# Four gated up projections: from 32 direct matmuls a chunk to seven block products, with the weight sums on GpSimd

## The chip, the cores and the metric

The kernel runs on one core of a Trainium2 chip, as one program written engine by engine: TensorE (PE), VectorE (DVE), ScalarE (ACT), GpSimd (POOL) and SyncE (SP) each have their own list of instructions, and they meet only at semaphores. The metric is the time of one execution on the device, in microseconds; lower is better. All arithmetic is in float32.

## The reference, cut to what matters

A sequence of 256 tokens with 1024 features goes through a first block of two layers and a second block of four layers. The change touches the gated feed-forward parts of the first block, two in each layer:

```python
def swiglu(h, w1, w3, w2):      # h: 256 x 1024, w1, w3: 1024 x 2816, w2: 2816 x 1024
    return (silu(h @ w1) * (h @ w3)) @ w2

mod = silu(c) @ w_ada[layer] + b_ada[layer]     # nine vectors of 1024 features
...
x = x + 0.5 * g1 * swiglu(modulate(rmsnorm(x), sh1, sc1), ffn_w1[layer, 0], ffn_w3[layer, 0], ffn_w2[layer, 0])
...                                             # attention
x = x + 0.5 * g3 * swiglu(modulate(rmsnorm(x), sh3, sc3), ffn_w1[layer, 1], ffn_w3[layer, 1], ffn_w2[layer, 1])
```

Each layer of the second block ends in a feed-forward part with a convolution over the gate (three taps). Its up projection has the same sizes.

## The kernel before

**Chunks.** All big weights come from memory in 244 chunks of 128 partitions x 4096 columns (2 MB), in the order of their use, through a ring of four slots. SyncE's queue issues them; the load of chunk c waits until chunk c - 4 is used (`chunks_used`). A chunk of an up projection holds, for eight blocks of 128 input features, 256 columns of w1 (the gate) and 256 columns of w3 (the up part). An up projection has 11 such chunks, j = 0 to 10; the down projection after it has 6.

**Gated stages.** There are four, n = 0 to 3 (`swiglu_pe`, `swiglu_act`, `swiglu_dve`, lines 1265 to 1308), at chunks 0, 26, 43 and 69. For each chunk TensorE multiplies its four column groups by the transposed tokens `hT` (eight blocks of 128 features x 256 tokens): 32 matmuls of 256 columns (`channels_pe`, line 600), into PSUM banks 4 and 5 for even j, 6 and 7 for odd j. The trace shows every float32 matmul as two records, so a chunk is 64. ScalarE takes the gate bank through SiLU into `cbuf` (line 1292), VectorE multiplies it by the up bank into `aT` (line 1308). Chunks 0 and 1 are multiplied token half by token half (128 columns), since the second half of `hT` comes later (`first_channels_pe`).

**Adaptive sums.** silu(c) @ w_ada is computed beside the stages 0, 1 and 2, in 36 pieces of 2 MB. VectorE runs over the eight 512-column blocks of a piece, one scaling and seven multiply-adds into `ada_sum` (lines 220 and 223), each with a wait for the one before. TensorE sums over the partitions with a matmul against ones (`ada_reduce_pe`, lines 231 and 234), and VectorE takes the result from PSUM (`ada_take_dve`, lines 250 to 263). Stages 0 and 1 carry eleven pieces, one a chunk, stage 2 seven, stage 3 none. TensorE reduces piece j - 1 just ahead of chunk j; VectorE sums piece j and takes piece j - 1 before the product of chunk j. The down projections 0 and 2 go on with pieces; they wait at their start until the pieces of the stage are taken (`ada_taken`).

**Stage 3** also normalizes the memory input (`mem_norm_act`, `mem_norm_dve`) at chunk 2 and transposes it on TensorE (`mem_pe`, line 638) at chunk 5.

**Block products elsewhere.** The up projections of the second block already use Strassen's form in Winograd's variant from chunk 2 on (`gated_pe`, lines 2590 to 2626): the chunk is a 2 x 2 matrix of blocks (halves of the input features by gate and up columns), `hT` too (feature halves by token halves), and seven products of 8 matmuls of 128 columns replace eight such products. VectorE forms the sums of weights, four operations of 128 x 1024 a chunk (`gated_left_dve`, lines 2573 to 2578), and adds the products up, seven operations of 128 x 256 (`gated_out_dve`, lines 2632 to 2641). The down projections 3, 5, 8, 11, 14 and the last use the form too (`seven_pe`, line 382).

**GpSimd** only sets up constants at the start and issues a few loads: small weights, gates and the memory (`attn_pool`, `gates_pool`, `mem_pool`, `mamba_pool`).

## Time and profile before

| what | value |
|---|---|
| median of 3 runs | 3718.9 us (3716.49 to 3721.02) |
| span of the profiled execution | 3717.0 us |
| instructions in it | 42263 |
| TensorE busy | 3667.4 us, 99% |
| VectorE busy | 1567.6 us, 42% |
| ScalarE busy | 736.1 us, 20% |
| GpSimd busy | 15.9 us |
| TensorE matmuls at line 600 (direct projections, these and others) | 5568 records, 941.6 us |
| HBM reads | 594.97 MB, 160 GB/s over the span |

The profile is one execution. "Busy" is the union of an engine's instructions; matmul ends are modelled. A line such as `L223 DVE SCALAR_TENSOR_TENSOR memT<-big,silu_c,memT 128x512 f32` names the source line, the engine, the operation, what it writes and reads, and the shape (partitions x elements). `x7` is the number of instructions merged. In the chain of waits each piece of time is put down to the instruction that ended last; when TensorE is 98% of it, the other engines matter only where they make it wait. The profile has no time for the work around the span apart from the runs' times; the median of the runs is 1.9 us above the span of this execution.

### The profile page before, as it was taken

What the parts mean: (1) busy time and instruction counts of PE and PEld (TensorE: products, weight loads), DVE (VectorE), ACT (ScalarE), POOL (GpSimd) and SP (SyncE); (2) the same over time, 40 slices, a digit from 0 to 9 for tenths busy, and PEclk for the clock granted to TensorE, in tenths of its full rate; (3) what the DMA queues carried; (4) which work ended last, traced back from release to release, by engine and by line L of the source; (5) the groups of instructions that cost most, each with busy time, mean ns of one, the idle gap of its engine ahead of it and who ended that gap; (6) DMA issues with size and microseconds to landing.
All of it is one profiled execution on the core that took longest, in us unless ns stands there. A gap on an engine that the chain in (4) does not pass through costs nothing.

```text
span 3717.0 us, 42263 instructions
## 1 busy us (share of the span) xinstructions
PE 3667.4 (99%) x18452; PEld 2737.0 (74%) x18452; DVE 1567.6 (42%) x2772; ACT 736.1 (20%) x1434; POOL 15.9 (0%) x43
## 2 busy tenths in 40 slices
PE   6999999999999999999999999999999999999999
PEld 5856697785668687587957679778657977757795
DVE  5434342334420345223833236736523673432384
ACT  1003400100431044211112111133211113521110
POOL 1000000000000000000000000000000000000000
PEclk9999999999999999999999999999999999999999
DMA  9753476554324442343443334432333444334342
GB/s 398 282 199 136 172 293 242 226 196 167 127 104 159 167 150 108 119 159 125 171 159 132 119 114 168 173 140 110 114 115 113 168 173 159 114 113 159 123 178 102
DMA packets 42472, 598.74 MB, mean 161 GB/s; under 512 B 4736, under 2 KB 4752, under 8 KB 6192
## 3 DMA queue, kind: packets, MB, share of 16 engines
q1 hardware_dynamic: 41024, 589.94, 42.9%
q0 software_dynamic: 1264, 6.10, 0.4%
q8 instruction: 146, 2.39, 0.3%
q14 instruction: 38, 0.31, 0.0%
HBM read 594.97 MB, written 1.05 MB: 160 GB/s over the span
## 4 chain that ended last, share of the span: by engine, by line
PE 98%; issue 1%; DVE 1%; ACT 1%; DMA 0%
PE ps L600 25%; PE ps L2602 12%; PE ps L483 9%; PE ps L382 8%; PE ps L463 5%; PE ps L2060 4%; PE ps L503 3%; PE ps L2093 3%; PE ps L796 3%; PE ps L2502 3%; PE ps L1568 2%; PE ps L1588 2%; PE ps L2829 2%; PE ps L1563 2%; PE ps L813 1%; PE ps L625 1%
## 5 line engine op out<-in xcount | busy, mean ns | idle before, releaser
L600 PE MATMUL ps<-hT,ring 128*128 128x256 f32 (+1 forms) x5568 | 941.6, 331 | 3.6 <-DVE stat L324 3.6
L600 PEld LDWEIGHTS ps<-hT,ring 128*128 128x128 f32 x5568 | 855.1, 191 | 88.1 <-issue 7.7
L483 PE MATMUL ps<-ring,aT 128*128 128x512 f32 x784 | 341.1, 592 | 0.0
L483 PEld LDWEIGHTS ps<-ring,aT 128*128 128x128 f32 x784 | 147.9, 190 | 179.1 <-issue 178.9
L463 PE MATMUL ps<-ring,aT 128*128 128x512 f32 x448 | 196.1, 597 | 0.0
L1308 DVE TENSOR_TENSOR aT<-cbuf,ps 128x512 f32<-128x512 f32 x44 | 30.3, 688 | 374.7 <-ACT cbuf L1292 374.7
L223 DVE SCALAR_TENSOR_TENSOR memT<-big,silu_c,memT 128x512 f32<-128x512 f32 x238 | 179.0, 752 | 8.5
L2060 PE MATMUL ps<-hT,ring 128*128 128x256 f32 x768 | 174.5, 384 | 0.0
L525 ACT ACTIVATE big<-x 128x1024 f32<-128x1024 f32 x34 | 35.9, 1057 | 696.6 <-DVE x L577 389.9
L2060 PEld LDWEIGHTS ps<-hT,ring 128*128 128x128 f32 x768 | 146.8, 193 | 26.7 <-issue 7.7
L463 PEld LDWEIGHTS ps<-ring,aT 128*128 128x128 f32 x448 | 85.1, 191 | 103.6 <-issue 103.5
L1292 ACT ACTIVATE cbuf<-ps 128x512 f32<-128x512 f32 x44 | 26.3, 597 | 579.1 <-PE ps L600 579.1
L2602 PE MATMUL ps<-big 128*128 128x128 f32 x1152 | 140.4, 275 | 0.0
L2602 PE MATMUL ps<-big,ring 128*128 128x128 f32 x1152 | 140.4, 275 | 0.0
L382 PE MATMUL ps<-ring,aT 128*128 128x512 f32 x288 | 135.3, 592 | 0.0
L2602 PE MATMUL ps<-hT,ring 128*128 128x128 f32 x1152 | 134.5, 275 | 0.0
L2602 PEld LDWEIGHTS ps<-big 128*128 128x128 f32 x1152 | 134.4, 192 | 0.0
L2602 PEld LDWEIGHTS ps<-big,ring 128*128 128x128 f32 x1152 | 134.4, 192 | 0.0
L2602 PEld LDWEIGHTS ps<-hT,ring 128*128 128x128 f32 x1152 | 131.5, 192 | 0.0
L2222 DVE SCALAR_TENSOR_TENSOR big<-cbuf,col,big 128x256 f32<-128x256 f32 x192 | 80.3, 480 | 101.9 <-ACT big L2109 100.7
L2093 PE MATMUL ps<-ring,hT 128*128 128x512 f32 x256 | 113.4, 594 | 0.0
L503 PE MATMUL ps<-big,ring 128*128 128x256 f32 x512 | 111.8, 379 | 0.0
(546 smaller groups left out, 4634.9 us busy)
## 6 DMA issues: line engine op xcount, KB each, us to landing
ring<-weights_in SPq DMA_DIRECT2D x244, 2048.0 KB, 7.7
big<-ada_in SPq DMA_DIRECT2D x34, 2048.0 KB, 7.8
ring<-ada_in SPq DMA_DIRECT2D x2, 2048.0 KB, 22.7
big<-b_gate_in POOLq DMA_DIRECT2D x1, 1536.0 KB, 17.3
x<-x_in SPq DMA_DIRECT2D x1, 1024.0 KB, 4.8
big<-b_gate_in POOLq DMA_DIRECT2D x1, 1024.0 KB, 8.9
big<-mem_in POOLq DMA_DIRECT2D x1, 1024.0 KB, 5.5
out<-big SPq DMA_DIRECT2D x2, 512.0 KB, 2.6
```

The source lines that it names most:

```text
L223: dve.scalar_tensor_tensor(out=ada_sum[:, a % 2, :], in0=w[:, k, :], scalar=silu_c[:, k:k + 1], in1=ada_sum[:, a % 2, :], op0=ALU.mult, op ...
L382: last = pe.matmul(ps[:, bank, :], left(2 * j + q), right[:, q, :], start=(j == 0 and q == 0), stop=(j == 3 and q == 1), skip_group_check= ...
L463: last = pe.matmul(ps[:, 2 * t + half, :], aT[:, 4 * j + k, t * P:(t + 1) * P], w[:, k, half * 512:(half + 1) * 512], start=(4 * j + k == ...
L483: last = pe.matmul(ps[:, 2 * t + half, :], aT[:, 4 * c + k, t * P:(t + 1) * P], w[:, k, half * 512:(half + 1) * 512], start=first, stop=(4 ...
L503: last = pe.matmul(ps[:, 4 + 2 * j + m // 2, (m % 2) * SEQ:(m % 2 + 1) * SEQ], w[:, k, m * P:(m + 1) * P], view(big, 0, KT, SEQ)[:, k, :], ...
L600: last = pe.matmul(ps[:, bank + m // 2, (m % 2) * SEQ + at:(m % 2) * SEQ + at + n], w[:, k, m * P:(m + 1) * P], hT[:, k, at:at + n], start ...
L796: last = pe.matmul(ps[:, bank + m // 2, (m % 2) * SEQ:(m % 2 + 1) * SEQ], w[:, k, m * P:(m + 1) * P], hT[:, k, :], start=(k == 0), stop=(k ...
L2060: last = pe.matmul(ps[:, bank + m // 2, (m % 2) * SEQ:(m % 2 + 1) * SEQ], w[:, k, m * P:(m + 1) * P], hT[:, k, :], start=(k == 0), stop=(k ...
L2093: last = pe.matmul(ps[:, 4 + 2 * (j % 2) + t, :], hT[:, k, t * P:(t + 1) * P], w[:, k, :], start=(k == 0), stop=(k == KT - 1))
L2222: last = dve.scalar_tensor_tensor(out=mamba_conv(j)[:, m, :], in0=cbuf[:, j % 2, m, 1 + tap:1 + tap + SEQ], scalar=col[:, w:w + 1], in1=ma ...
L2502: last = pe.matmul(cross_block(place), left[:, k, :], right[:, k, :], start=(k == 0), stop=(k == 3), skip_group_check=True)
L2602: last = pe.matmul(gated_block(j, place)[:, m * P:(m + 1) * P], left[:, k, m * P:(m + 1) * P], right[:, k, :], start=(k == 0), stop=(k == ...
```

## The change

From chunk 2 on, each gated stage uses the seven products. The four sums of weights are on GpSimd (`up_left_pool`), into three single buffers of `big` and in place in the ring; the four sums of `hT` on VectorE once a stage (`up_right_dve`); the sums of products on VectorE, seven operations of 128 x 256 a chunk (`up_out_dve`). ScalarE copies product 1 from PSUM into `cbuf` and takes SiLU of the finished gate in place. The product of gate and up reads both from SBUF. Even chunks use banks 4 to 6 and half of bank 3, odd chunks banks 0 to 2 and the other half of bank 3; bank 7 is for the adaptive reductions. A reduction now stands between the fourth and the fifth product of its chunk and waits until the piece before it is taken (`taken=0`); the take stands behind the sums of the chunk's products, and then comes the sum of the next piece but one. The down projections 0 and 2 wait for the last product of the stage already at their first reduction; down projections 3 and 5 wait for the sums of products of chunk 10 before their third product. The memory's norm comes at the start of stage 3, its transposes before chunk 2. The wait counts of the later stages are shifted for the semaphores that are now shared (gated_left by 144, gated_out by 180, gated_products, seven_tokens); nothing else changes there.

```diff
-        def ada_reduce_pe(pe, a, bank):
+        def ada_bank(bank):
+
+            return ps[:, bank, :]
+
+        def ada_reduce_pe(pe, a, place, taken=1):
 
             pe.wait_ge(ada_step, 8 * a + 8)
             if a >= 4:
-                pe.wait_ge(ada_taken, a - 1)
+                pe.wait_ge(ada_taken, a - taken)
...
                 if j < len(ada):
-                    ada_reduce_pe(pe, ada[j], 6 + ada[j] % 2)
+                    if j == 0:
+                        pe.wait_ge(*then)
+                    ada_reduce_pe(pe, ada[j], ada_bank(6 + ada[j] % 2))
...
+        def up_left_part(i):
+
+            return view(big, 12288 + 1024 * i, 4, SEQ)
+
+        def up_right_part(i):
+
+            return (view(big, 15360, 4, P), view(big, 15872, 4, P), view(gdn_work, 512, 4, P), view(aTf, 5120, 4, P))[i]
+
+        def up_block(j, at):
+
+            if at == 6 and j < 10:
+                return ps[:, 3, SEQ * (1 - j % 2):SEQ * (1 - j % 2) + SEQ]
+            return ps[:, 4 * (1 - j % 2) + at // 2, SEQ * (at % 2):SEQ * (at % 2) + SEQ]
+
+        def up_ada_place(j):
+
+            return ps[:, 7, SEQ:512] if j == 10 else ps[:, 7, :]
...
+        def up_ready(engine, i):
+
+            if i is None:
+                engine.wait_ge(norm_act_done, 5)
+                engine.wait_ge(norm_dve_done, 7)
+            else:
+                engine.wait_ge(down_act_done, 6 * i + 6)
+                engine.wait_ge(down_dve_done, 8 * i + 8)
+
+        def up_left_pool(pool, n, i, c0):
+
+            s1, s2, s4 = (up_left_part(part) for part in range(3))
+            up_ready(pool, i)
+            for j in range(2, 11):
+
+                w = arrived(pool, c0 + j).rearrange("p (k c) -> p k c", k=KT)
+                a11, a12, a21, a22 = w[:, 0:4, 0:SEQ], w[:, 4:8, 0:SEQ], w[:, 0:4, SEQ:512], w[:, 4:8, SEQ:512]
+                if j > 2:
+                    pool.wait_ge(gated_products, up_products_count(n, j - 1, 2))
+                pool.tensor_tensor(s1, a21, a22, ALU.add).then_inc(gated_left, 1)
+                pool.wait_ge(gated_left, up_left_count(n, j, 1))
+                pool.tensor_tensor(a21, a11, a21, ALU.subtract).then_inc(gated_left, 1)
+                if j > 2:
+                    pool.wait_ge(gated_products, up_products_count(n, j - 1, 3))
+                pool.tensor_tensor(s2, s1, a11, ALU.subtract).then_inc(gated_left, 1)
+                if j > 2:
+                    pool.wait_ge(chunks_used, c0 + j)
+                pool.wait_ge(gated_left, up_left_count(n, j, 3))
+                pool.tensor_tensor(s4, a12, s2, ALU.subtract).then_inc(gated_left, 1)
+
+        def up_right_dve(dve, n, i):
+
+            b11, b12, b21, b22 = hT[:, 0:4, 0:P], hT[:, 0:4, P:SEQ], hT[:, 4:8, 0:P], hT[:, 4:8, P:SEQ]
+            t1, t2, t3, t4 = (up_right_part(part) for part in range(4))
+
+            up_ready(dve, i)
+            dve.tensor_tensor(t1, b12, b11, ALU.subtract).then_inc(seven_tokens, 1)
+            dve.tensor_tensor(t3, b22, b12, ALU.subtract).then_inc(seven_tokens, 1)
+            dve.wait_ge(seven_tokens, up_right_count(n) + 1)
+            dve.tensor_tensor(t2, b22, t1, ALU.subtract).then_inc(seven_tokens, 1)
+            dve.wait_ge(seven_tokens, up_right_count(n) + 3)
+            dve.tensor_tensor(t4, b21, t2, ALU.subtract).then_inc(seven_tokens, 1)
+
+        def up_pe(pe, n, c0, j, ada, mem):
+
+            w = arrived(pe, c0 + j).rearrange("p (k c) -> p k c", k=KT)
+            s1, s2, s4 = (up_left_part(part) for part in range(3))
+            t1, t2, t3, t4 = (up_right_part(part) for part in range(4))
+
+            def product(place, left, right):
+                for m in range(2):
+                    for k in range(4):
+                        last = pe.matmul(up_block(j, place)[:, m * P:(m + 1) * P], left[:, k, m * P:(m + 1) * P], right[:, k, :], start=(k == 0), stop=(k == 3), skip_group_check=True)
+                return last
+
+            if j >= 4:
+                pe.wait_ge(gated_out, up_out_count(n, j - 2, 5))
+            elif j == 2:
+                pe.wait_ge(swiglu_dve_done, 11 * n + 1)
+            product(1, w[:, 4:8, 0:SEQ], hT[:, 4:8, 0:P])
+            product(0, w[:, 0:4, 0:SEQ], hT[:, 0:4, 0:P]).then_inc(gated_products, 1)
+            pe.wait_ge(seven_tokens, up_right_count(n) + 4)
+            pe.wait_ge(gated_left, up_left_count(n, j, 1))
+            product(2, s1, t1).then_inc(gated_products, 1)
+            if j == 2:
+                pe.wait_ge(swiglu_dve_done, 11 * n + 2)
+            product(4, w[:, 4:8, SEQ:512], t4)
+            for a in ada:
+                ada_reduce_pe(pe, a, up_ada_place(j), taken=0)
+            pe.wait_ge(gated_left, up_left_count(n, j, 3))
+            product(3, s2, t2).then_inc(gated_products, 1)
+            if j > 2:
+                pe.wait_ge(gated_out, up_out_count(n, j - 1, 4))
+            elif mem:
+                pe.wait_ge(mem_act_done, 4)
+                pe.wait_ge(mem_dve_done, 4)
+            product(6, w[:, 0:4, SEQ:512], t3)
+            pe.wait_ge(gated_left, up_left_count(n, j, 4))
+            product(5, s4, hT[:, 4:8, P:SEQ]).then_inc(chunks_used, 1)
+
+        def up_out_dve(dve, n, c0, j):
+
+            p1, p2, p5, p6, p4, p3, p7 = (up_block(j, at).rearrange("p (m c) -> p m c", m=2) for at in range(7))
+            part, late = view(gdn_work, 0, 2, P), view(gdn_work, 256, 2, P)
+            gate, up = cbuf[:, j % 2, 0:2, 4:260], aT[:, 2 * j:2 * j + 2, :]
+
+            dve.wait_ge(chunks_used, c0 + j + 1)
+            dve.wait_ge(swiglu_act_done, up_act_count(n, j, 1))
+            dve.tensor_tensor(part, gate[:, :, 0:P], p6, ALU.add).then_inc(gated_out, 1)
+            dve.tensor_tensor(gate[:, :, 0:P], gate[:, :, 0:P], p2, ALU.add)
+            dve.wait_ge(gated_out, up_out_count(n, j, 1))
+            dve.tensor_tensor(late, part, p5, ALU.add).then_inc(gated_out, 1)
+            dve.wait_ge(gated_out, up_out_count(n, j, 2))
+            dve.tensor_tensor(gate[:, :, P:SEQ], late, p3, ALU.add).then_inc(gated_out, 1)
+            dve.tensor_tensor(part, part, p7, ALU.add).then_inc(gated_out, 1)
+            dve.wait_ge(gated_out, up_out_count(n, j, 4))
+            dve.tensor_tensor(up[:, :, P:SEQ], part, p5, ALU.add)
+            dve.tensor_tensor(up[:, :, 0:P], part, p4, ALU.add).then_inc(gated_out, 1)
+
         def swiglu_pe(pe, n, i, c0, ada=(), mem=False):
 
             if i is None:
                 pe.wait_ge(norm_dve_done, 8)
+                for j in range(2):
+                    w = arrived(pe, c0 + j).rearrange("p (k c) -> p k c", k=KT)
+                    channels_pe(pe, w, 4 + 2 * j).then_inc(chunks_used, 1)
+            else:
+                first_channels_pe(pe, i, c0)
+            if mem:
+                mem_pe(pe)
+            for a in ada[0:1]:
+                ada_reduce_pe(pe, a, ada_bank(0))
+            for j in range(2, 11):
+
+                up_pe(pe, n, c0, j, ada[j - 1:j], mem)
...
+        def swiglu_act(act, n, c0, mem=False):
+
+            if mem:
+                mem_norm_act(act)
             for j in range(11):
 
-                if j and j - 1 < len(ada):
-                    ada_reduce_pe(pe, ada[j - 1], ada[j - 1] % 4)
-                if mem and j == 5:
-                    mem_pe(pe)
+                if mem and j == 2:
+                    mem_take_act(act)
+                gate = cbuf[:, j % 2, 0:2, 4:260]
                 if j >= 2:
-                    pe.wait_ge(swiglu_dve_done, 11 * n + j - 1)
-                if j == 0 and i is not None:
-                    first_channels_pe(pe, i, c0)
-                elif j > 1 or i is None:
-                    w = arrived(pe, c0 + j).rearrange("p (k c) -> p k c", k=KT)
-                    channels_pe(pe, w, 4 + 2 * (j % 2)).then_inc(chunks_used, 1)
-
-        def swiglu_act(act, n, c0, mem=False):
-
+                    act.wait_ge(gated_products, up_products_count(n, j, 1))
+                    act.wait_ge(swiglu_dve_done, 11 * n + j - 1)
+                    act.copy(gate[:, :, 0:P], up_block(j, 0).rearrange("p (m c) -> p m c", m=2)).then_inc(swiglu_act_done, 1)
+                    act.wait_ge(gated_out, up_out_count(n, j, 3))
+                    act.activation(gate, gate, ACT.Silu).then_inc(swiglu_act_done, 1)
+                else:
+                    act.wait_ge(chunks_used, c0 + j + 1)
+                    act.activation(gate, ps[:, 4 + 2 * j, :].rearrange("p (m c) -> p m c", m=2), ACT.Silu).then_inc(swiglu_act_done, 1)
+
+        def swiglu_dve(dve, n, i, c0, ada=(), mem=False, seven=None):
+
+            if mem:
+                mem_norm_dve(dve)
+            up_right_dve(dve, n, i)
+            for a in ada[0:1]:
+                ada_sum_dve(dve, a)
             for j in range(11):
 
                 if mem and j == 2:
-                    mem_norm_act(act)
-                if mem and j == 5:
-                    mem_take_act(act)
-
-                act.wait_ge(chunks_used, c0 + j + 1)
+                    mem_take_dve(dve)
                 if j >= 2:
-                    act.wait_ge(swiglu_dve_done, 11 * n + j - 1)
-                act.activation(cbuf[:, j % 2, 0:2, 4:260], ps[:, 4 + 2 * (j % 2), :].rearrange("p (m c) -> p m c", m=2), ACT.Silu).then_inc(swiglu_act_done, 1)
-
-        def swiglu_dve(dve, n, c0, ada=(), mem=False, seven=None):
-
-            for j in range(11):
-
-                if mem and j == 2:
-                    mem_norm_dve(dve)
-                if mem and j == 5:
-                    mem_take_dve(dve)
-
-                if j < len(ada):
-                    ada_sum_dve(dve, ada[j])
-                if j and j - 1 < len(ada):
-                    ada_take_dve(dve, ada[j - 1], ada[j - 1] % 4)
-                dve.wait_ge(swiglu_act_done, 11 * n + j + 1)
-                dve.tensor_tensor(aT[:, 2 * j:2 * j + 2, :], cbuf[:, j % 2, 0:2, 4:260],
-                                  ps[:, 5 + 2 * (j % 2), :].rearrange("p (m c) -> p m c", m=2), ALU.mult).then_inc(swiglu_dve_done, 1)
+                    up_out_dve(dve, n, c0, j)
+                    for a in ada[j - 1:j]:
+                        ada_take_dve(dve, a, up_ada_place(j))
+                    for a in ada[j + 1:j + 2]:
+                        ada_sum_dve(dve, a)
+                dve.wait_ge(swiglu_act_done, up_act_count(n, j, 1 if j < 2 else 2))
+                if j >= 2:
+                    dve.wait_ge(gated_out, up_out_count(n, j, 5))
+                up = aT[:, 2 * j:2 * j + 2, :] if j >= 2 else ps[:, 5 + 2 * j, :].rearrange("p (m c) -> p m c", m=2)
+                dve.tensor_tensor(aT[:, 2 * j:2 * j + 2, :], cbuf[:, j % 2, 0:2, 4:260], up, ALU.mult).then_inc(swiglu_dve_done, 1)
+                if j < 2:
+                    for a in ada[0:j]:
+                        ada_take_dve(dve, a, ada_bank(0))
+                    for a in ada[j + 1:j + 2]:
+                        ada_sum_dve(dve, a)
 
                 if seven is not None and j >= 7:
                     seven_left_dve(dve, seven, j - 7, swiglu_dve_done, 11 * n + 2 * (j - 7) + 2)
...
             attn_pool(pool, 0)
+            up_left_pool(pool, 0, None, c0=0)
+            attn_pool(pool, 1)
             gates_pool(pool, 0)
-            attn_pool(pool, 1)
+            up_left_pool(pool, 1, 1, c0=26)
             gates_pool(pool, 1)
+            up_left_pool(pool, 2, 2, c0=43)
             mem_pool(pool)
             mamba_pool(pool, (attn_dve_done, 4), layer=0)
+            up_left_pool(pool, 3, 4, c0=69)
             gdn_pool(pool)
             mamba_pool(pool, (mix_dve_done, 8), layer=1)
             last_pool(pool)
...
-            down_pe(pe, 3, (swiglu_dve_done, 32), c0=54, nk=22, then=(swiglu_dve_done, 33), seven=0, taken=(swiglu_act_done, 33))
+            down_pe(pe, 3, (swiglu_dve_done, 32), c0=54, nk=22, then=(swiglu_dve_done, 33), seven=0, taken=(gated_out, up_out_count(2, 10, 5)))
```

## Rows read from the trace of the kernel before

**Rows 1.** The page: engines' busy time, granted TensorE clock, chain by engine.

```profile
PE 3667.4 (99%) x18452; PEld 2737.0 (74%) x18452; DVE 1567.6 (42%) x2772; ACT 736.1 (20%) x1434; POOL 15.9 (0%) x43
...
PEclk9999999999999999999999999999999999999999
...
PE 98%; issue 1%; DVE 1%; ACT 1%; DMA 0%
```

**Rows 2.** The chain in order of time: start us, us, what.

```profile
1166.43 82.88 PE ps L600 x384
...
1748.67 112.56 PE ps L2602 x1008
```

**Rows 3.** Windows, stages 0 to 3 (chunks 2 to 10) and a convolutional one.

```profile
core 0: us, PE busy (x) PEld busy (x) DVE busy (x) ACT busy (x) POOL busy (x), PEclk, DMA share, GB/s
73.06:205.32 132.26, 132.26 (x631) 115.94 (x630) 60.11 (x93) 5.38 (x10) 0.00 (x0) 1.00 0.80 295
485.10:617.48 132.38, 132.38 (x637) 116.54 (x637) 60.38 (x97) 4.78 (x8) 0.00 (x0) 1.00 0.81 302
724.21:854.68 130.47, 130.47 (x615) 114.15 (x614) 46.75 (x77) 5.37 (x10) 0.00 (x0) 1.00 0.56 210
1123.28:1249.35 126.07, 126.07 (x593) 111.14 (x592) 18.03 (x32) 11.60 (x21) 0.00 (x0) 1.00 0.41 150
1748.66:1861.22 112.56, 112.56 (x1010) 112.56 (x1009) 90.35 (x155) 18.33 (x44) 0.00 (x0) 1.00 0.46 169
```

**Rows 4.** Timeline, memory transposes in stage 3.

```profile
1164.52 1.91 PE L638 MATMUL ps<-ident,big 128*128 128x128 f32 x16
```

**Rows 5.** Timeline of a chunk of stage 0: start us, us, instruction.

```profile
191.24 0.69 DVE L1308 TENSOR_TENSOR aT<-cbuf,ps 128x512 f32<-128x512 f32 x1 [8.03 <-ACT cbuf L1292]
191.85 0.48 DVE L220 TENSOR_SCALAR memT<-big,silu_c 128x512 f32<-128x512 f32 x1
192.37 5.48 DVE L223 SCALAR_TENSOR_TENSOR memT<-big,silu_c,memT 128x512 f32<-128x512 f32 x7
197.76 0.15 DVE L259 TENSOR_TENSOR modc<-ps,col 128x4 f32<-128x4 f32 x1
```

**Rows 6.** Timeline of a convolutional stage, VectorE's sums of products.

```profile
1773.72 0.42 DVE L2632 TENSOR_TENSOR cbuf<-big,ps 128x256 f32<-128x256 f32 x1 [2.75 <-PE ps L2602]
...
1776.09 0.41 DVE L2641 TENSOR_TENSOR gdn_work<-gdn_work,ps 128x256 f32<-128x256 f32 x1
1776.42 1.79 DVE L2690 SCALAR_TENSOR_TENSOR aT<-cbuf,col,aT 128x256 f32<-128x256 f32 x4
```

**Rows 7.** Groups by line and shape, VectorE: busy us, mean ns.

```profile
L2573 DVE TENSOR_TENSOR big<-ring 128x1024 f32<-128x1024 f32 x36 | 43.9, 1219 | 0.0
...
L588 DVE TENSOR_SCALAR big<-x,stat 128x1024 f32<-128x1024 f32 x34 | 25.6, 753 | 1.2
...
L2705 DVE TENSOR_TENSOR aT<-aT,gdn_work 128x512 f32<-128x512 f32 x36 | 24.6, 684 | 0.0
```

**Rows 8.** Timeline, first two products (four records each) of down projection 3.

```profile
854.48 1.88 PE L382 MATMUL ps<-ring,aT 128*128 128x512 f32 x4
...
856.19 1.88 PE L382 MATMUL ps<-ring,big 128*128 128x512 f32 x4
```

**Rows 9.** Timeline, GpSimd.

```profile
1.46 0.20 POOL L172 MEMSET gt<- 128x128 f32 x1
1.60 0.20 POOL L172 MEMSET ge<- 128x128 f32 x1
...
5.30 0.29 POOL L165 TENSOR_SCALAR_AFFINE_SELECT gt<-gt 128x128 f32<-128x128 f32 x1
5.55 0.29 POOL L165 TENSOR_SCALAR_AFFINE_SELECT ge<-ge 128x128 f32<-128x128 f32 x1
...
2572.46 0.95 POOL L1202 MEMSET big<- 128x1024 f32 x1 [474.83 <-PE ps L750]
```

**Rows 10.** Timeline, GpSimd's load of the last gates.

```profile
696.27 0.54 POOL L1925 DMA_DIRECT2D big<-b_gate_in  x1 [238.99 <-DVE big L580]
```

76 lines of the change are left out of this document (43 added, 33 removed).

## The prediction, made before the change was run

> **What bounds the kernel now.** I read the page's engine and chain lines first. TensorE is busy for 99% of the span, 98% of the chain that ended last is TensorE, and its granted clock stands at the top digit in every slice [rows 1]. So a shorter matmul stream shortens the kernel by just what it removes, as long as TensorE is not made to wait. Next I read the chain in order of time: six up-projection chunks in the direct form take 82.88 us, 13.81 each, and the nine chunks of a convolutional stage, which already run as seven block products, take 112.56 us, 12.51 each [rows 2]. Last I read the windows of chunks 2 to 10 in each gated stage: 132.3, 132.4, 130.5 and 126.1 us, TensorE busy in all of it, VectorE in 60, 60, 47 and 18 us, GpSimd in none [rows 3]. What these hold above nine times 13.81 us is the reduction of the adaptive-norm sums: (132.26 - 124.3) / 9 = 0.9 us a chunk.
>
> All sums below are made against the profiled span of 3717.0 us; the median of the runs is 3718.9, so I add a difference to the median. 0.2% of it, 7.4 us, is about what a measurement of this kernel can tell from no change.
>
> **What TensorE saves.** Per chunk 64 records of 256 columns become 112 of 128. That is the form of the convolutional stage, same engine, same shapes, so its row gives the price: 13.81 - 12.51 = 1.30 us a chunk, 36 chunks, 46.8 us. The reductions stay (9, 9, 6 and 0 in these windows), only moved to the middle of a chunk, 0.9 us each. A chunk with one is then 12.5 + 0.9 = 13.4 us. In the fourth stage the transposes of the memory (1.9 us, [rows 4]) move from chunk 5 to chunk 2; same price, the norm work they wait for now comes at the stage's start, under the 20 us of chunks 0 and 1. Undelayed windows: 120.5, 120.5, 118.8 and 114.5 us.
>
> **What VectorE gets.** A chunk with an adaptive sum costs it now 0.61 us (product, start to start) plus 5.91 (eight steps of the sum, 191.85 to 197.76) [rows 5]. Added are seven 128x256 sums out of PSUM. Their pattern stands in the convolutional stage: 1773.72 to 1776.42, 2.70 us [rows 6]. With the take at 0.35 (mean of 0.2 to 1.1) and about 0.25 for new waits: 2.70 + 0.35 + 5.91 + 0.60 + 0.25 = 9.8 us. That is below 13.4, so by itself it is hidden. The product's operand moves from PSUM to SBUF: 0.68 us in the convolutional stage against 0.69 [rows 5, 7], nothing. The right-hand sums (four of 128x512, once a stage, some 2.6 us) lie under chunks 0 and 1.
>
> **What the order costs at the end of a stage.** The sums of chunk 10 can begin only when TensorE has finished it. In stages 0 and 1 the down projection waits until take number nine is in, and that take now stands behind these sums: 0.2 + 2.7 + 0.35 = 3.3 us of idle TensorE, where before the take was long done. VectorE's queue holds nothing else there. In stages 2 and 3 the down projection runs two products, 1.71 us each [rows 8], before it wants the sums of chunk 10: 3.4 us cover 2.9, no cost (up to 1 us if the hand-over is slow). Together 2 x 3.3 = 6.6 us. That price is bounded by nothing (were the take earlier) and about 5 us (were a scaled take of 1.1 us there and a slow hand-over).
>
> **What GpSimd gets.** Four 128x1024 two-input sums a chunk, T us each. The trace has no such operation. Nearest rows [rows 9]: a memset of the size takes 0.95 us and only writes; memsets of 128 columns start 0.15 us apart, selects of 128 (one input) 0.25, so reading adds 0.10 per 128 or 0.8 per 1024. Write plus two reads is 0.95 + 0.8 + 0.8 = 2.5; the select times eight is 2.0. Outer ends: 0.95 (reads free) and 4.0 (each input as dear as the whole select). I take 2.25. Then 4T = 9.0 us, under the 12.5 of a chunk. The buffers are single: sums 1 and 3 of the next chunk may start when product three of this one is done (5.4 us into it), the second after product five, the fourth at the chunk's end, and is needed 10.7 us later. All fit up to T of 3.1 (3.35 with a reduction), and then GpSimd sets the pace. On its own queue nothing urgent stands behind: the load of the last gates now follows stage 1's sums, but it waited until 696 us anyway, and stage 1 ends at 617 [rows 3, 10]. Each chunk's DMA must land one chunk earlier for GpSimd than for TensorE; the ring is four deep and the DMA share is 0.80 in the densest window [rows 3], 0.88 at 13.4 us a chunk, so I price it at nothing (up to 1 us a chunk in stages 0 and 1 if the transfers were to bind at that share). SP's order of issues is unchanged; each adaptive load is issued some 3 us later in the chunk and has a whole chunk to spare.
>
> **The choice: do the two engines run side by side?** This decides the sign. In the trace of before GpSimd never reads SBUF while VectorE runs a two-input operation, so no row tells. Below: they do not touch each other. Above: one holds the other for a whole instruction.
>
> If they exclude each other, VectorE's 9.8 us hold 3.1 us (sums and take, which read PSUM and one SBUF operand) that can lie beside GpSimd, and 6.7 that cannot. GpSimd's 9.0 us can hide only 3.1. The period becomes 9.8 + 9.0 - 3.1 = 15.7 us, against 14.70 before, and TensorE feels it through the take, for which the next reduction waits in mid-chunk. Stages 0 and 1: first chunk 13.4, eight periods 125.6, end 3.3, total 142.3 against 132.3: +10.0 each. Stage 2 has only four such periods: the sums of chunk 6 start at 13.4 + 62.8 = 76.2, chunk 7's reduction can start at 79.3 and the chunk ends at 79.3 + 0.9 + 5.4 (three products) = 85.6 instead of 80.4, so 118.8 + 5.2 = 124.0 against 130.5: -6.5. Stage 3 has no adaptive sums: 114.5 against 126.1: -11.6. Sum +1.8 us, 3720.7. With T = 2.0 the period is 14.7: +4.0 - 10.5 - 11.6 = -18. With T = 2.5 it is 16.7: +36 - 2.5 - 11.6 = +22. This case's own range is 3701 to 3741.
>
> The Trainium skill has a rule for this very pair (SBUF — State Buffer, Who interferes with whom): VectorE and GpSimd share one port pair, and a VectorE instruction with two SBUF inputs and a GpSimd instruction that reads SBUF block each other for their full length, while one with at most one SBUF input does not. No row here shows it or speaks against it. Its GPSIMD Engine Reference (3.1 Elementwise) gives 4497 ns for a two-input add of 2048 columns; an estimate from that page is 2.25 us for 1024, and the sum by it would be the one above.
>
> I take the exclusion as the likeliest case. The nearest sign in the rows is that VectorE scales 1024 columns of one SBUF operand in 0.75 us, but adds two such operands in 1.22 [rows 7]: with two inputs it seems to use up a path that it can otherwise spend on speed, and the change puts a second two-input reader beside it.
>
> **Rivals.**
> A. The engines do not disturb each other. For it: nothing in the trace shows a conflict, and both engines' loads alone (9.8 and 9.0 us) fit in a chunk. The gain is 46.8 - 6.6 = 40.2 us: 3679.
> B. The exclusion above, the forecast: 3721, no change that a measurement can tell. For it: VectorE and GpSimd work add up to more than a chunk. Against: it needs whole-instruction blocking.
> C. Slower: GpSimd becomes the bound by itself, from T = 3.35 on. At T = 4.0 each of the 36 chunks takes 16.0 us: 144 us a window, +15, +15, +13.5 and +18 with the ends: 3780. For it: the select's rate, twice. Against: the memset's rate. The same time comes out if VectorE's PSUM sums were held too (period 9.8 + 9.0 = 18.8, +50 us over B).
> D. Partial disturbance, both stretched but inside 13.4 to 14.7 us: 3690 to 3715.
>
> **How the numbers follow.** B 0.55, A 0.30, C 0.08, D 0.07. Faster by over 0.2% (below 3711.5): all of A, most of D, and the quarter of B with T under 2.13: 0.30 + 0.05 + 0.13 = 0.48. Within 0.2%: 0.20 of B and a bit of D, 0.22. Slower: the rest of B, with T above 2.34, and C: 0.22 + 0.08 = 0.30. The range of 3674 to 3744 leaves out C and the edges of the rest.
>
> **What would show it.** In the profile after: L2602-like products at 112 records and 12.5 us a chunk (the saving); the GpSimd adds' start-to-start spacing (T); the vector multiply-adds of 0.75 us stretched to 2 us and more beside GpSimd adds, and chunk ends 15.7 us apart in stages 0 and 1 (B) or at 0.75 us and 13.4 (A); TensorE idle before the middle of a chunk on VectorE's take; 3.3 us of idle before the first down products of stages 0 and 1. The forecast fails if the multiply-adds keep their 0.75 us, or if T is outside 2.0 to 2.5.

## The result, and the profile after

| kernel | median us | runs | span profiled |
|---|---|---|---|
| before | 3718.9 (3714.8 to 3721.6) | 8 | 3717.0 |
| after | 3728.3 (3725.0 to 3730.7) | 8 | 3726.5 |

The ratio is 1.0027, interval 1.0017 to 1.0036. The change makes the kernel about 9 us slower. The forecast was 3721, inside a case of its own from 3701 to 3741, and the case was the right one: GpSimd and VectorE hold each other off. The loss is about 7 us larger than forecast.

The page of the profile after, the lines that answer to [rows 1]: busy time, granted clock, the chain by engine, and the group of VectorE's multiply-adds.

```profile
PE 3641.1 (98%) x20180; PEld 2766.1 (74%) x20180; DVE 1831.5 (49%) x3040; ACT 745.8 (20%) x1468; POOL 375.3 (10%) x187
...
PEclk9999999999999999999999999999999999999999
...
PE 88%; DVE 9%; issue 1%; ACT 1%; DMA 0%; DVEq 0%
...
L223 DVE SCALAR_TENSOR_TENSOR memT<-big,silu_c,memT 128x512 f32<-128x512 f32 x238 | 295.6, 1242 | 8.4
```

TensorE is busy 26 us less than before (3641.1 against 3667.4) and yet the span grew. VectorE has moved into the chain, 9% where it had 1%. It also has 264 us more to do, and 116.6 us of that is no new work: the 238 multiply-adds of the modulations are the same instructions as before, at 1242 ns each where they took 752. The row of the chain that answers to [rows 2] is that of stage 3, which has no modulations:

```profile
1146.80 112.56 PE ps L1358 x1008
```

Nine chunks in 112.56 us, 12.51 each, to the hundredth what the convolutional stage takes. The saving itself is real: the question is only what takes it back.

The windows of the four stages after, columns as in [rows 3]; the last window is part of a chunk of stage 0:

```profile
72.64:210.30 137.66, 126.30 (x1063) 123.87 (x1062) 130.80 (x160) 8.35 (x18) 80.51 (x32) 0.96 0.71 281
491.00:633.90 142.90, 127.72 (x1079) 125.76 (x1077) 137.20 (x166) 8.94 (x19) 81.70 (x32) 0.96 0.75 301
742.40:876.40 134.00, 124.91 (x1049) 122.27 (x1048) 105.08 (x137) 8.54 (x18) 79.81 (x32) 0.95 0.60 233
1144.90:1259.40 114.50, 114.50 (x1027) 114.49 (x1026) 37.21 (x85) 10.28 (x22) 74.97 (x32) 1.00 0.45 166
139.70:147.10 7.40, 7.35 (x40) 7.38 (x41) 7.15 (x9) 0.00 (x0) 1.81 (x1) 0.59 1.00 392
```

In stages 0 and 1 VectorE is busy 95 and 96% of the window: it, not TensorE, sets the pace. TensorE stands still for 11 to 15 us of each. In stage 3 it never waits. The granted clock of TensorE (a share of its full clock), 1.00 in every window of [rows 3], is 0.96, 0.96 and 0.95 in stages 0 to 2, and 0.59 in the short last window; the experiment with extra matmuls comes back to it.

The mechanism can be read in one chunk of stage 0. The timeline: start us, us, instruction.

```profile
89.49 0.43 DVE L258 TENSOR_SCALAR big<-big 128x512 f32<-128x512 f32 x1
...
89.83 0.48 DVE L220 TENSOR_SCALAR memT<-big,silu_c 128x512 f32<-128x512 f32 x1
90.35 13.35 DVE L223 SCALAR_TENSOR_TENSOR memT<-big,silu_c,memT 128x512 f32<-128x512 f32 x7
...
91.67 2.42 POOL L1325 TENSOR_TENSOR big<-ring 128x1024 f32<-128x1024 f32 x1 [2.73 <-PE ps L1358]
...
94.17 2.68 POOL L1327 TENSOR_TENSOR ring<-ring 128x1024 f32<-128x1024 f32 x1
...
96.81 2.79 POOL L1330 TENSOR_TENSOR big<-big,ring 128x1024 f32<-128x1024 f32 x1
...
99.75 2.61 POOL L1334 TENSOR_TENSOR big<-ring,big 128x1024 f32<-128x1024 f32 x1
...
105.07 2.36 POOL L1325 TENSOR_TENSOR big<-ring 128x1024 f32<-128x1024 f32 x1 [2.71 <-PE ps L1358]
105.33 0.42 DVE L1399 TENSOR_TENSOR cbuf<-gdn_work,ps 128x256 f32<-128x256 f32 x1
```

Seven multiply-adds, 5.48 us in [rows 5], take 13.35 beside four of GpSimd's sums: 7.9 us longer, 84% of four times 2.35. The sums of products at 105.33 and after, which read PSUM and one SBUF operand, keep their 0.42 us beside the same GpSimd instruction. What the prediction's sum left out is that an instruction with one SBUF input can be held too. The timeline, a little later:

```profile
122.02 2.35 POOL L1327 TENSOR_TENSOR ring<-ring 128x1024 f32<-128x1024 f32 x1
...
122.28 2.37 DVE L220 TENSOR_SCALAR memT<-big,silu_c 128x512 f32<-128x512 f32 x1
...
122.51 1.02 PE L238 MATMUL ps<-ones,memT 128*128 128x1 f32 x8 [1.79 <-DVE modc L263]
```

The scaling that takes 0.48 us at 89.83 takes 2.37 here: it ends 0.3 us after GpSimd's sum does. And TensorE has stood for 1.79 us before the reduction, waiting for the take.

Where the 9.5 us of span came from, read at the first matmul of each down projection in the two timelines (us; the intervals hold what lies between two of them, so the stages' chunks 2 to 10 are in the first, third, fourth and last). The last three columns are experiments, told further on:

| interval that ends at down projection | before | after | same kernel again | memsets | chunks 3, 5, 7, 8, 9 |
|---|---|---|---|---|---|
| 0 (stage 0) | 205.12 | 210.32 | 213.66 | 195.56 | 198.54 |
| 1 | 219.96 | 221.73 | 221.67 | 221.70 | 219.96 |
| 2 (stage 1) | 192.20 | 201.90 | 203.45 | 183.67 | 185.67 |
| 3 (stage 2) | 237.20 | 242.34 | 237.66 | 227.20 | 228.25 |
| 4 | 209.58 | 209.59 | 209.59 | 209.59 | 209.58 |
| 5 (stage 3) | 185.09 | 173.32 | 173.32 | 173.32 | 173.33 |

After minus before: +5.2, +1.8, +9.7, +5.1, 0, -11.8: +10.0 in all. Two executions of the changed kernel differ by 3.3, 1.6 and 4.7 us in stages 0 to 2: which of VectorE's instructions meets which of GpSimd's, and where the clock falls, is not the same each time.

### The profile page after: what moved, and what is told of

It reads as the page before. It is cut to its first block, busy times and chain, and to the rows that moved or that the text cites. A ratio compares the mean times of both kernels' runs of the same rounds, so it can differ in the third digit from the quotient of the medians.

```text
span 3726.5 us, 46342 instructions
## 1 busy us (share of the span) xinstructions
PE 3641.1 (98%) x20180; PEld 2766.1 (74%) x20180; DVE 1831.5 (49%) x3040; ACT 745.8 (20%) x1468; POOL 375.3 (10%) x187
## 4 chain that ended last, share of the span: by engine, by line
PE 88%; DVE 9%; issue 1%; ACT 1%; DMA 0%; DVEq 0%
PE ps L2760 12%; PE ps L606 11%; PE ps L489 9%; PE ps L386 8%; PE ps L1358 6%; DVE memT L223 5%; PE ps L467 5%; PE ps L2218 4%; PE ps L509 3%; PE ps L2251 3%; PE ps L802 3%; PE ps L2660 3%; PE ps L1726 2%; PE ps L1746 2%; PE ps L2987 2%; PE ps L1721 2%
## 5 line engine op out<-in xcount | busy, mean ns | idle before, releaser
L606 PE MATMUL ps<-hT,ring 128*128 128x128 f32 (+1 forms) x3264 | 438.3, 297 | 3.6 <-DVE stat L328 3.6
L606 PEld LDWEIGHTS ps<-hT,ring 128*128 128x128 f32 x3264 | 418.7, 192 | 26.1 <-issue 3.8
L223 DVE SCALAR_TENSOR_TENSOR memT<-big,silu_c,memT 128x512 f32<-128x512 f32 x238 | 295.6, 1242 | 8.4
L2218 PEld LDWEIGHTS ps<-hT,ring 128*128 128x128 f32 x768 | 144.7, 190 | 25.8 <-issue 7.6
L1358 PE MATMUL ps<-big 128*128 128x128 f32 x1152 | 152.8, 290 | 0.0
L1358 PEld LDWEIGHTS ps<-big 128*128 128x128 f32 x1152 | 145.9, 205 | 3.9 <-issue 3.9
L2760 PE MATMUL ps<-big 128*128 128x128 f32 x1152 | 140.4, 275 | 0.0
L1358 PE MATMUL ps<-hT,ring 128*128 128x128 f32 x1152 | 134.6, 275 | 0.0
L2760 PE MATMUL ps<-hT,ring 128*128 128x128 f32 x1152 | 134.5, 275 | 0.0
L2760 PEld LDWEIGHTS ps<-big 128*128 128x128 f32 x1152 | 134.4, 192 | 0.0
L1358 PEld LDWEIGHTS ps<-hT,ring 128*128 128x128 f32 x1152 | 131.7, 192 | 1.0 <-issue 1.0
L2760 PEld LDWEIGHTS ps<-hT,ring 128*128 128x128 f32 x1152 | 131.5, 192 | 0.0
```

The source lines that it names most:

```text
L223: dve.scalar_tensor_tensor(out=ada_sum[:, a % 2, :], in0=w[:, k, :], scalar=silu_c[:, k:k + 1], in1=ada_sum[:, a % 2, :], op0=ALU.mult, op ...
L606: last = pe.matmul(ps[:, bank + m // 2, (m % 2) * SEQ + at:(m % 2) * SEQ + at + n], w[:, k, m * P:(m + 1) * P], hT[:, k, at:at + n], start ...
L1358: last = pe.matmul(up_block(j, place)[:, m * P:(m + 1) * P], left[:, k, m * P:(m + 1) * P], right[:, k, :], start=(k == 0), stop=(k == 3), ...
L2218: last = pe.matmul(ps[:, bank + m // 2, (m % 2) * SEQ:(m % 2 + 1) * SEQ], w[:, k, m * P:(m + 1) * P], hT[:, k, :], start=(k == 0), stop=(k ...
L2760: last = pe.matmul(gated_block(j, place)[:, m * P:(m + 1) * P], left[:, k, m * P:(m + 1) * P], right[:, k, :], start=(k == 0), stop=(k == ...
```

## Experiments

**Write-only GpSimd.** What of GpSimd disturbs VectorE, and is it the whole loss?

```diff
-pool.tensor_tensor(s1, a21, a22, ALU.add).then_inc(gated_left, 1)
+pool.memset(s1, 0.0).then_inc(gated_left, 1)
+pool.wait_ge(gated_left, up_left_count(n, j, 1) - 1)
+pool.memset(s1, 0.0).then_inc(gated_left, 1)      # the other three sums likewise
```

> Each of GpSimd's 144 sums of weights is replaced by two memsets of the same 1024 columns (0.95 us each in the kernel before), with the same waits and signals; they read nothing, so the block products work on zeros and the output is not the reference's. GpSimd stays active for about 1.9 us per sum, in the same places. Theory 1 (GpSimd's reads and VectorE's operations with two SBUF inputs, or one in the fast form, hold each other off for whole instructions): the multiply-adds go back from 1242 ns to 0.75 to 0.80 us, the chunks of stages 0 and 1 come every 13.4 us, and the time is case A of the prediction, 3679 (3672 to 3690). Rival 2 (any GpSimd activity, its writes or its semaphores, slows VectorE): the multiply-adds stay above 1.1 us and the time near 3720 to 3728. Rival 3 (the order of VectorE's work, not the length of its operations, holds the stages): the multiply-adds shorten, but the chunks of stages 0 and 1 still come every 15 us or more.

Measured: 3677.7, 3680.7 and three times 3689.2 us; ratio to before 0.9909 (0.9893 to 0.9924). Its group of multiply-adds, and its timeline at the same chunk:

```profile
L223 DVE SCALAR_TENSOR_TENSOR memT<-big,silu_c,memT 128x512 f32<-128x512 f32 x238 | 178.9, 752 | 8.5
```

```profile
89.75 5.47 DVE L223 SCALAR_TENSOR_TENSOR memT<-big,silu_c,memT 128x512 f32<-128x512 f32 x7
...
91.04 0.95 POOL L1325 MEMSET big<- 128x1024 f32 x1 [3.46 <-PE ps L1366]
92.05 0.95 POOL L1327 MEMSET big<- 128x1024 f32 x1
...
93.06 0.95 POOL L1329 MEMSET ring<- 128x1024 f32 x1
...
94.07 0.95 POOL L1331 MEMSET ring<- 128x1024 f32 x1
```

Four memsets run right beside the seven multiply-adds, and these take 5.47 us. Over the kernel 752 ns, as before to the nanosecond. So it is neither GpSimd's activity nor its writes nor the semaphores. The sums of products of stage 0 begin 13.4 us apart (85.60, 99.00, 112.40 and so on), as TensorE alone would have it, so it is not the order of VectorE's work either. Each affected interval falls: against before -9.6, -8.5 and -10.0 us, and -11.8 in stage 3. This is case A of the prediction come true in all but its premise, and its price is right as well: 3679 forecast, 3677.7 to 3680.7 in the executions that had no trouble elsewhere. Where the other 10 us of three executions come from stands in the last section: they arise far behind the stages that were changed. One limit: two memsets fill 1.9 us of the 2.4 that a sum takes, so this GpSimd is also about a fifth less busy.

**One input in place of two.** Is it the second input of GpSimd's sums that shuts VectorE out, or any reading?

```diff
-pool.tensor_tensor(s1, a21, a22, ALU.add)
+pool.tensor_copy(s1, a21)      # the other three likewise
```

> Each of GpSimd's sums of weights is replaced by a copy of its first operand (one SBUF input in place of two, 1024 columns, same waits and signals); the block products then work on wrong weights and the output is not the reference's. If any read of GpSimd holds off VectorE's operations with two SBUF inputs, the multiply-adds stay above 0.75 us, by as much as the copies last. If only GpSimd's operations with two inputs do, they are back at 0.75 and the time is that of the run with memsets, 3678 to 3689.

Measured: 3679.1, 3679.5, 3688.7 and 3688.7; ratio 0.9902 (0.9888 to 0.9916). The same chunk in its timeline:

```profile
89.40 7.44 DVE L223 SCALAR_TENSOR_TENSOR memT<-big,silu_c,memT 128x512 f32<-128x512 f32 x7
...
90.71 1.13 POOL L1325 COPY big<-ring 128x1024 f32<-128x1024 f32 x1 [4.39 <-PE ps L1358]
91.90 1.38 POOL L1327 COPY ring<-ring 128x1024 f32<-128x1024 f32 x1
...
95.11 1.19 POOL L1330 COPY big<-big 128x1024 f32<-128x1024 f32 x1 [1.83 <-PE ps L1358]
```

5.47 has become 7.44: 1.97 us more beside three copies of together 3.7. So one input is enough; over the kernel the multiply-adds average 887 ns. But a copy lasts 1.08 to 1.27 us where a sum lasts 2.35, VectorE is busy 76% of stage 0's window, and in this trace TensorE never waits for a take inside a stage. The first reading of the expectation holds for the duration, the second for the time. That GpSimd reads is not enough to make the change lose; how long it reads decides. What the second input adds is more than length: 1.97 us are 53% of the copies' 3.7, where the sums added 84% of theirs. No run separates the two.

**The take ahead of the sums.** The other explanation of the lost time is order: the take for which TensorE waits stands behind 2.7 us of sums.

```diff
+for a in ada[j - 1:j] if j < 10 else ():
+    ada_take_dve(dve, a, up_ada_place(j))
 up_out_dve(dve, n, c0, j)
-for a in ada[j - 1:j]:
+for a in ada[j - 1:j] if j == 10 else ():
     ada_take_dve(dve, a, up_ada_place(j))
```

> In chunks 2 to 9 VectorE takes the reduced modulation first and then sums the products, so the reduction of the next chunk no longer waits for the 2.7 us of those sums; nothing else is changed. Theory 1 (VectorE's stretched operations fill the period: 131.4 of 138.3 us busy in stage 0, 137.2 of 142.9 in stage 1): at most the idle rest can be won, 6.9 and 5.7 us; the period stays above 15 us, time 3716 to 3729. Rival 3 (the order holds TensorE): 2.7 us come off each of some 16 periods, about 3685.

Measured: 3732.5 us, ratio 1.0033 (1.0021 to 1.0046). Nothing won; the 3685 of the order theory is ruled out, and 3732.5 lies even 3 us over what theory 1 gave. In its trace the idle of TensorE before down projections 0 and 2 has grown to 5.18 and 5.39 us. Its windows of stages 0 and 1:

```profile
72.00:210.00 138.00, 127.24 (x1066) 124.46 (x1064) 135.05 (x152) 8.20 (x18) 82.67 (x32) 0.96 0.68 268
491.00:634.00 143.00, 132.35 (x1108) 130.19 (x1107) 139.17 (x158) 8.09 (x18) 83.59 (x32) 0.94 0.71 281
```

VectorE is at 98 and 97%. An engine that is as full as here gives its result in the same period whatever it does first.

**The changed kernel again**, for a second trace and a second comparison.

> The changed kernel, unchanged, beside the others on one chip, so that the runs with the take first and with extra matmuls (3732.5, 3732.0 and 3731.3 us) have it in their own comparison: 3728 (3725 to 3731).

Measured: 3728.9 (3724.7 to 3730.3), ratio 1.0025 (1.0015 to 1.0034), so take-first (1.0033) and the two kernels that follow (1.0034 and 1.0033) can't be told from it by their times. It ran on another chip than they did, so only these ratios, each to runs of before on the same chip, can be compared.

**Extra matmuls in the wait.** After some waits TensorE ran at a lower clock. The timeline after, in stage 0 and at the start of down projection 0:

```profile
137.25 2.34 POOL L1327 TENSOR_TENSOR ring<-ring 128x1024 f32<-128x1024 f32 x1
...
137.62 1.99 DVE L267 SCALAR_TENSOR_TENSOR modc<-modc,col 128x4 f32<-128x4 f32 x1
...
139.75 1.83 PE L238 MATMUL ps<-ones,memT 128*128 128x1 f32 x8 [3.60 <-DVE modc L267]
...
141.45 3.76 PE L1358 MATMUL ps<-big 128*128 128x128 f32 x16
...
145.00 2.29 PE L1358 MATMUL ps<-gdn_work,ring 128*128 128x128 f32 x16
...
147.13 1.95 PE L1358 MATMUL ps<-hT,big 128*128 128x128 f32 x16
```

```profile
210.32 15.67 PE L467 MATMUL ps<-ring,aT 128*128 128x512 f32 x32 [2.87 <-issue]
```

TensorE had stood for 3.60 us; then 16 matmuls took 3.76 us where 1.95 is usual, about the lower of the clock's two levels, 1.2 and 2.4 GHz (the last window above, 0.59, holds these matmuls and some at the full clock). The wait itself was stretched by GpSimd too: the last step of this take, four columns from two SBUF operands, took 1.99 us where it takes 0.16 undisturbed. To see whether the standing still does it, it was filled:

```diff
 if ada:
+    for _ in range(7):      # 3 in the second run
+        pe.matmul(ps[:, 0, :], ones[:, :], hT[:, 0:2, :].rearrange("p k c -> p (k c)"), start=True, stop=True, skip_group_check=True)
     pe.wait_ge(ada_taken, ada[0])
```

> At the start of the down projections 0 and 2, ahead of the wait for the last take, seven extra 128x512 matmuls of 0.21 us into a free bank (1.5 us in all, less than the 2.9 and 3.1 us of the wait). Theory 4 (the granted clock falls because TensorE had stood still, and stays at the lower level over the next chunk): these two chunks of the down projection return from 15.7 and 15.6 to 13.7 us, 3.8 us less in all, 3724.5. Rival (the chunk is slow from what runs beside it, or the clock doesn't care for a wait of 1.5 us less): within 1 us of 3728.

> As the run with seven extra matmuls, but with three, 0.88 us each by that run's trace (6.17 us for seven): 2.6 us, within the 2.9 and 3.1 us of the two waits. Theory 4: no time is added, and the first chunk of the down projections 0 and 2 takes 13.9 us in place of 15.7 and 15.6: 3.5 us less than the full change, 3725. Rival: the chunk stays at 15.6.

The first was mis-sized: a 128x512 matmul of this type takes 0.88 us and not 0.21, and seven of them took 6.17 us, more than the wait. The timeline of the second at the same place:

```profile
207.65 2.74 PE L458 MATMUL ps<-hT,ones 128*128 128x512 f32 x6
210.62 14.00 PE L469 MATMUL ps<-ring,aT 128*128 128x512 f32 x32 [0.24 <-DVE modc L263]
```

14.00 us in place of 15.67 (13.90 with seven): the interval to down projection 1 is 220.07 and 219.96, where the full change has 221.73 and before 219.96. But the second trace of the changed kernel, where nothing fills the same wait, shows this:

```profile
213.66 13.97 PE L467 MATMUL ps<-ring,aT 128*128 128x512 f32 x32 [2.87 <-issue]
```

So a wait of 2.87 us need not cost the clock. (The 221.67 us of this interval in that trace contain a loss of 1.6 us elsewhere, near 430 us.) Counted over the traces: behind the unfilled waits of 2.87 and 3.06 us at the start of down projections 0 and 2 the first chunk took 15.5 to 15.7 us in seven of eight cases (the changed kernel twice, memsets, copies); with the wait filled it took 13.9 to 14.0 in four of four; behind the waits of 1.53 and 1.72 us of the kernels further down the clock stayed at 1.00 in eight of eight. The price, 1.6 to 1.8 us a time, follows the idle engine, but not every time. The time as a whole, 3732.0 and 3731.3 us, did not show the 3.5 us. In the trace with three matmuls interval 1 is 1.7 us shorter than after, but stage 1 is 1.8 longer, and another 1.7 is lost behind stage 3; whether the other executions lose it the same way is not shown.

**Stages alone.** Block products in stage 3 only, then in stages 2 and 3 only. A chunk without them is computed directly, with its reduction between the column groups:

```diff
+BLOCKED = ((), (), (), (2, 3, 4, 5, 6, 7, 8, 9, 10))      # then (), (), all, all
+if j not in BLOCKED[n]:      # in up_pe: four column groups of 128
+    ...
+    return                   # and so on in the other engines' loops
```

> Block products in stage 3 alone; stages 0 to 2 as in the kernel before, with the reduction between the column groups. If the stages don't act on each other, the time is the kernel before less stage 3's 11.8 us: 3707 (3705 to 3709). If part of what stage 3 seems to win is work that the late stages before it have pushed out of it, the win is smaller: over 3710.

> Block products in all chunks of stages 2 and 3, none in stages 0 and 1 (direct form, with its 1.53 and 1.72 us at their ends). The stage forecast wrongly was stage 2: -6.5 us, and it took 3.4 us more. If that comes from within stage 2 (its first chunks' sums beside GpSimd's), it is there again: 3.4 - 11.8 + 3.3 = 5 us less than before, 3714 to 3716. If it was inherited from the late stages ahead, stage 2 now gives its -6.5: 3704 to 3706.

Stage 3 only: 3711.7, ratio 0.9976 (0.9967 to 0.9986), 8 us less than before. Stage 3's interval is 173.33, the full 11.8 us. The rest of the difference is the direct form itself: its reduction comes later in the last chunk, so down projections 0 and 2 begin with idles of 1.53 and 1.72 us; and interval 4 is 211.22 us where all others have 209.59, a clock loss near 1070 us (granted 0.91 over 20 us). Stages 2 and 3: 3710.1, ratio 0.9980 (0.9972 to 0.9989), between what the two expectations gave. Stage 2's interval is 236.20, 1.0 us less than before, not -6.5 and not +3.4. So most of what was missed arises in the stage. Carried over for certain is only the slow first chunk of the down projection ahead of it, 1.7 us, which this kernel does not have; without it the second trace of the full change has -1.1 in this interval and the first +3.4, so what is left between them is scatter from one execution to the next. In the trace of this run the modulation that VectorE sums in chunk 1 of stage 2 is already stretched, since GpSimd begins with the weights of chunk 3 before VectorE has come to chunk 2 (its sums of products begin at 746.84):

```profile
733.37 13.55 DVE L224 SCALAR_TENSOR_TENSOR memT<-big,silu_c,memT 128x512 f32<-128x512 f32 x7
...
734.18 2.35 POOL L1337 TENSOR_TENSOR big<-ring 128x1024 f32<-128x1024 f32 x1 [15.06 <-PE ps L1370]
```

**Fewer chunks.** If VectorE is simply full, block products pay in as many chunks as it has room for.

```diff
+BLOCKED = ((3, 4, 6, 7, 9), (3, 4, 6, 7, 9), (3, 4, 6, 7, 8, 9, 10), (2, ..., 10))      # first
+BLOCKED = ((3, 5, 7, 9), (3, 5, 7, 9), (3, 5, 7, 8, 9, 10), (2, ..., 10))               # second
```

> Block products only in chunks 3, 4, 6, 7 and 9 of stages 0 and 1, in chunks 3, 4, 6, 7, 8, 9 and 10 of stage 2 and in all nine of stage 3, 26 chunks in all; the other chunks are computed directly, with the reduction between their column groups (in the run with stage 3 alone this form cost 1.53 and 1.72 us at the ends of stages 0 and 1). Theory 1: VectorE's work per chunk is 6.9 us for a direct chunk and 9.8 for one of block products, plus at most the 9.6 us of GpSimd's four sums: over nine chunks of stage 0 at most 4 x 6.9 + 5 x 19.4 = 125 us against TensorE's 9 x 14.7 - 5 x 1.3 = 126, so it just fits: 26 x 1.30 = 33.8 us saved less 3.3 lost, 3689 (3686 to 3696). If two chunks of block products in a row don't fit (2 x 19.4 = 38.8 against 2 x 13.4 and the slack of one chunk), some waits of 2 to 4 us stay and it comes out above 3696.

> As the last, but never two chunks of block products in a row while modulations are summed: chunks 3, 5, 7 and 9 of stages 0 and 1, chunks 3, 5, 7, 8, 9 and 10 of stage 2, all of stage 3, 23 in all. Theory 1: each pair needs at most 6.9 + 19.4 = 26.3 us of VectorE against 28.1 of TensorE, so no wait is left: 23 x 1.30 = 29.9 us saved less 3.3, 3693 (3690 to 3697). If it was not GpSimd's overlap that cost time but the block products' own work beside the modulations, each of the 14 chunks in stages 0 to 2 still loses some of the 2.5 us that it lost in the full change: above 3700.

Measured: 3691.3 (ratio 0.9928, 0.9914 to 0.9942) and 3691.5 (0.9923, 0.9910 to 0.9935). Both are faster than before by 28 us, as theory 1 had it. With two chunks in a row TensorE still waits 2.5 us in all for takes, with alternating ones not at all; both still stand for 1.53 and 1.72 us at the ends of stages 0 and 1. Then, in the chunks computed directly, with the take ahead of VectorE's product of gate and up, against that idle:

```diff
+BLOCKED = ((3, 5, 7, 9), (3, 5, 7, 9), (3, 4, 6, 7, 8, 9, 10), (2, ..., 10))            # third
+BLOCKED = ((3, 5, 7, 8, 9), (3, 5, 7, 8, 9), (3, 4, 6, 7, 8, 9, 10), (2, ..., 10))      # fourth
+if j >= 2 and j not in BLOCKED[n]:
+    for a in ada[j - 1:j]:
+        ada_take_dve(dve, a, up_ada_place(j))      # taken out behind the product
```

> Block products in chunks 3, 5, 7 and 9 of stages 0 and 1, in 3, 4, 6, 7, 8, 9 and 10 of stage 2 and in all of stage 3, 24 chunks; in the chunks computed directly VectorE takes the modulation before it multiplies the chunk, so that the down projections no longer wait behind that (1.53 and 1.72 us). Theory 1: 24 x 1.30 = 31.2 us less than the kernel before and no wait at the ends, 3688.5 (3686 to 3691). If the wait at the ends was for something else, 3.3 us more.

> As the last, with block products in chunk 8 of stages 0 and 1 too. No modulation is summed after chunk 8, so VectorE has room behind it: 26 x 1.30 = 33.8 us less, 3686 (3683 to 3689). If chunks 7, 8 and 9 in a row are already too much for VectorE, waits of 2 to 4 us before the last modulations give the 2.6 us back: 3688 or more.

Measured: 3686.8 (0.9924, 0.9909 to 0.9940; two of six executions took 3698.3) and 3687.0 (0.9913, 0.9900 to 0.9926). The idle at the ends is gone in both. The windows of stages 0 and 1 of the fourth, and its multiply-adds:

```profile
72.00:210.00 138.00, 137.52 (x898) 122.88 (x897) 99.95 (x139) 7.33 (x15) 42.88 (x17) 1.00 0.79 309
491.00:634.00 143.00, 143.00 (x885) 120.30 (x884) 87.54 (x123) 7.29 (x14) 40.96 (x16) 1.00 0.75 296
```

```profile
L224 DVE SCALAR_TENSOR_TENSOR memT<-big,silu_c,memT 128x512 f32<-128x512 f32 x238 | 240.3, 1010 | 8.4
```

The multiply-adds are still a third longer than before, and it costs next to nothing: VectorE is busy 72 and 61% of the windows and TensorE 99.7 and 100%, at full clock. Its intervals fall by 6.6, 6.5, 9.0 and 11.8 us, that is five, five, seven and nine times 1.30. In the sum to down projection 5 that is 33.8 us, what 26 chunks should save. These two are the fastest kernels that compute the reference, some 33 us under before, and can't be told apart. The fourth keeps 72% of the 46.8 us with 26 of 36 chunks.

## Why the prediction was right, point by point

- **The saving**, 1.30 us a chunk: right, 12.51 us a chunk in stage 3, and the four mixed kernels followed it.
- **The choice, that the engines exclude each other**: right. The memsets show that GpSimd's reading is what stretches VectorE's instructions and that this is the whole loss. The prediction drew here on the Trainium skill (SBUF — State Buffer, Who interferes with whom). The traces agree for VectorE's instructions with two SBUF inputs, for those that read PSUM and one SBUF operand (0.42 us undisturbed), and for GpSimd's writes, which don't count. The section says too that VectorE's fast two-port forms contend, a scaling among them, even with one SBUF input. I had left that exception out of the rule and of the sum, and the trace bears it out (0.48 us became 2.37). I had also put the takes among the work that can lie beside GpSimd, as reading PSUM and one SBUF operand. That holds for their first step only; 20 of the 36 have a second step that reads only SBUF, and some of these were held as well (0.16 us became 1.99 in the timeline above, 0.43 became 1.72 in stage 2). Of GpSimd's full length 84% came on top in the group shown, not all of it.
- **T, a GpSimd sum**: 2.25 us taken. In the run with stage 3 alone, where VectorE hardly disturbs, the four groups average 2.35 to 2.40 us; with the full change 2.48 to 2.56. The Trainium skill's figure (GPSIMD Engine Reference, 3.1 Elementwise), halved, was 2.25 as an estimate, some 5% low.
- **The period of 15.7 us in stages 0 and 1**: in stage 0 the sums of products begin at 86.20 us and, seven periods on, at 197.56: 15.9 each; in stage 1 from 510.02 to 619.71, 15.7 each. Right in size, though by two errors that offset each other: T is 0.1 us more than taken and the blocking less than whole. The eighth period is 9.9 and 11.2 us, not 15.7, GpSimd having nothing left to add: a term that I had overlooked. Stage 0 lost 5.2 us where +10.0 stood (8.5 in the second execution); stage 1 lost 9.7 (11.3) for +9.9.
- **The ends of stages 0 and 1**, 3.3 us each: 2.87 and 3.06 measured. Right, a little less; missing was the clock behind them, another 1.6 to 1.8 us in three of the four cases in the two traces.
- **Stage 2, -6.5 us**: the step that failed. Its interval grew by 5.1 us; in the second execution by 0.5. I counted four stretched periods, from chunk 2 on, and these came as forecast: from 761.29 to 824.78 us, 63.5 for 62.8. What I left out lies before and behind them. Before: the down projection ahead had its slow first chunk, 1.7 us. And the sum that VectorE makes in chunk 1 already runs beside GpSimd's work for chunk 3 and takes 13.35 us where 5.48 is usual:

```profile
748.02 13.35 DVE L223 SCALAR_TENSOR_TENSOR memT<-big,silu_c,memT 128x512 f32<-128x512 f32 x7
...
761.29 0.42 DVE L1394 TENSOR_TENSOR gdn_work<-cbuf,ps 128x256 f32<-128x256 f32 x1
```

  So the first sums of products begin 127.3 us behind the first matmul of down projection 2, where in the run with memsets it is 122.95: 4.4 us late. Behind: chunk 7, forecast to end 9.4 us after the sums of chunk 6 begin (3.1 until the reduction, 0.9 and 5.4), ended after 14.2 (838.97). The take that came there is one of the long ones and its second step was held, so the reduction began 5.1 us behind the sums and not 3.1; and the lower clock behind that wait of 3.87 us cost another 2.6. With seven chunks of block products in place of nine the same stage gained all its 9.0 us: it has room for seven, and I had counted on nine.
- **Stage 3, -11.6**: -11.8.
- **Rivals**: A (no disturbance, 3679) is out as a description but its price was met by the memsets to within 2 us. C (GpSimd the bound) is out: T is 2.4, and GpSimd works in 80 of 138 us. D (a partial disturbance, within the chunk's slack) is out for this kernel: the stages' periods are 15.7 to 15.9 us. The copies come nearest to it, stretched by a part of their length and inside the chunk, at a better time (3679 to 3689) than D gave.

The total was 7 us off. The forecast called it no change that a measurement can tell; what came is a loss of 0.27% with an interval that leaves out no change, an outcome that had been given 0.30. By intervals, measured against forecast: stage 0 -4.8, down projection 0 +1.8 (clock, no term of mine), stage 1 -0.2, stage 2 +11.6, stage 3 -0.2, together +8.2 on a sum of +1.8. That it came so near owes something to luck, since stage 0 and stage 2 were wrong in opposite directions; in the second execution stage 0 is only 1.5 below its forecast and stage 2 7.0 above. The clock was lost behind seven waits within stages as well, for about 1.5 to 1.7 us of matmul time at four of them and 2.4 to 2.7 at three; how much of that reached the time is not shown, since VectorE sets the pace there.
